# Turning the normalised rows of a one-core transformer kernel: scaled rows and transposes in place of a product with a diagonal

## What is computed

```python
def rms_norm(x, g, eps=NORM_EPS):
    xf = x.astype(F32)
    y = xf * lax.rsqrt(jnp.mean(xf * xf, axis=-1, keepdims=True) + eps)
    return (y * g.astype(F32)).astype(x.dtype)

for layer in range(DEPTH_2):
    h = swiglu_ffn(rms_norm(x, g[0]), ffn_w_gu[layer, 0], ffn_w_down[layer, 0])
    x = x + HALF_STEP * rms_norm(h, g[1])
    h = rms_norm(x, g[2])
    ...
    x = x + rms_norm(h, g[3])
    h = swiglu_ffn(rms_norm(x, g[4]), ffn_w_gu[layer, 1], ffn_w_down[layer, 1])
    x = x + HALF_STEP * rms_norm(h, g[5])
```

## Time and profile before

| | |
|---|---|
| median of 3 runs | 2836.6 us (2833.71 to 2836.64) |
| profiled execution, its own time | 2834.07 us |
| its span | 2832.3 us |
| mean granted TensorE clock | 0.981 |
| TensorE matmul busy | 2712.9 us, 96%, 19782 records |
| VectorE busy | 1760.8 us, 62% |
| ScalarE busy | 1419.7 us, 50% |
| GpSimd busy | 138.0 us, 5% |

### The profile page before, as it was taken

How to read it: one execution, slowest core, us unless ns; L and a number is a source line. 1 busy time by engine, 2 the same in 40 slices (tenths; PEclk the granted TensorE clock), 3 DMA queues, 4 the chain that set the end, 5 groups by cost and what they waited for, 6 DMA issues and landing times.

```text
span 2832.3 us, 47861 instructions
## 1 busy us (share of the span) xinstructions
PE 2712.9 (96%) x19782; PEld 2445.5 (86%) x19782; DVE 1760.8 (62%) x2118; ACT 1419.7 (50%) x1872; POOL 138.0 (5%) x206
## 2 busy tenths in 40 slices
PE   7899999899999999988998999999999999999999
PEld 7789999788888888878897888889988888888887
DVE  5555788665556665568655656566656566555655
ACT  5544577544545455456324445444345455455544
POOL 3000000000000000000301000000000000000000
PEclk9989999999999999999999999999999999999999
DMA  7165899555535545543203555555445545553553
GB/s 204 44 216 173 277 354 352 190 193 182 155 122 178 185 167 201 187 146 105 92 4 105 190 181 195 188 183 174 155 155 190 188 168 196 193 157 106 184 188 124
DMA packets 371293, 491.97 MB, mean 174 GB/s; under 512 B 12313, under 2 KB 331377, under 8 KB 371121
## 3 DMA queue, kind: packets, MB, share of 16 engines
q1 hardware_dynamic: 367968, 479.51, 50.5%
q0 software_dynamic: 2576, 7.97, 1.0%
q10 hardware_dynamic: 576, 1.98, 0.2%
HBM read 488.38 MB, written 1.05 MB: 173 GB/s over the span
## 4 chain that ended last, share of the span: by engine, by line
PE 88%; DVE 5%; ACT 4%; issue 1%; POOL 1%; DMA 0%; ACTq 0%; POOLq 0%; DVEq 0%
PE bank L351 21%; PE bank L350 11%; PE bank L330 9%; PE bank L331 9%; PE bank L332 9%; PE acc L330 7%; PE acc L332 7%; PE acc L331 7%; PE bank L2872 1%; ACT w_hi L295 1%; PE acc L604 1%; DVE X L509 1%; PE bank L2849 1%; DVE act_both L530 1%; PE bank L2860 1%
## 5 line engine op out<-in xcount | busy, mean ns | idle before, releaser
L300 DVE TENSOR_TENSOR w_lo<-raw,w_hi 128x2048 fp32r<-128x2048 f32 x360 | 824.1, 2292 | 509.7 <-ACT w_hi L295 509.2
L295 ACT ACTIVATE w_hi<-raw 128x2048 fp32r<-128x2048 f32 x360 | 688.2, 1912 | 268.6 <-PE acc L332 229.2
L351 PE MATMUL bank<-act_both,w_hi 128*128 128x512 f32 x2560 | 654.7, 392 | 0.0
L351 PEld LDWEIGHTS bank<-act_both,w_hi 128*128 128x128 f32 x2560 | 465.2, 189 | 82.8
L350 PEld LDWEIGHTS bank<-act_both,w_lo 128*128 128x128 f32 x2560 | 349.1, 190 | 25.0
L330 PE MATMUL acc<-w_hi,mix_hi 128*128 128x512 f32 x928 | 363.8, 392 | 4.4 <-ACT att_probs L1175 2.2
L332 PE MATMUL acc<-w_hi,mix_lo 128*128 128x512 f32 x928 | 362.0, 390 | 0.0
L331 PE MATMUL acc<-w_lo,mix_hi 128*128 128x512 f32 x928 | 361.7, 390 | 0.0
L350 PE MATMUL bank<-act_both,w_lo 128*128 128x256 f32 x2560 | 356.8, 282 | 0.0
L738 ACT ACTIVATE scratch<-bank 128x256 f32<-128x256 f32 x320 | 122.3, 385 | 429.1 <-PE bank L351 422.6
L330 PE MATMUL bank<-act_both,w_hi 128*128 128x256 f32 x1032 | 298.8, 290 | 22.1 <-DVEq L2290 8.0
(11 more groups left out here) (512 smaller groups left out, 3867.3 us busy)
## 6 DMA issues: line engine op xcount, KB each, us to landing
raw<-in_ffn_w_gu SPq DMA_DIRECT2D x176, 1024.0 KB, 5.0
raw<-in_ffn_w_down SPq DMA_DIRECT2D x88, 1024.0 KB, 4.8
raw<-in_ml_w_in SPq DMA_DIRECT2D x24, 1024.0 KB, 5.2
raw<-in_rt_w_in SPq DMA_DIRECT2D x24, 1024.0 KB, 5.1
raw<-in_w_up SPq DMA_DIRECT2D x20, 1024.0 KB, 6.8
raw<-in_w_gate SPq DMA_DIRECT2D x19, 1024.0 KB, 6.3
raw<-in_w_down SPq DMA_DIRECT2D x18, 1024.0 KB, 6.0
moe_raw<-in_w_down SPq DMA_DIRECT2D x14, 1024.0 KB, 6.0
```

Source lines behind the costliest of these rows:

```text
L295: act.activation(w_hi[0:rows, slot, 0:size], raw[0:rows, slot, 0:size], ACT.Copy).then_inc(hi_made, 1)
L300: dve.tensor_tensor(w_lo[0:rows, slot, 0:size], raw[0:rows, slot, 0:size], w_hi[0:rows, slot, 0:size].bitcast(F32), ALU.subtract).then_inc ...
L351: return pe.matmul(bank[b][:, :], w_hi[:, slot, w], act_both[:, k, :], start=k == 0, stop=k == KT - 1)
```

## The change

ScalarE no longer makes a diagonal. `spread(t)` multiplies the row half `X[:, t]` by `rstd`, in two instructions of 512 columns, into `scratch[:, t]`, each with its own count on the semaphore `rows_scaled`. TensorE turns `scratch` with the transpose form of the matmul against the identity, and waits before k = 0 for the first half and before k = 4 for the second.

```diff
--- before.py
+++ after.py
@@ -196,7 +196,6 @@
         scratch = sb("scratch", [P, TT, D])
         silu_out = sb("silu_out", [P, 2, 2 * T])
         gated = sb("gated", [P, 2, 2 * T])
-        diag = gated[:, 0, 0:TT * P].rearrange("p (t c) -> p t c", t=TT)
         work0 = top[0]
         assert work0 < nc.sbuf_usable_end
 
@@ -227,7 +226,7 @@
         x_quarter = sem("x_quarter")
         x_summed_act, x_summed_dve = sem("x_summed_act"), sem("x_summed_dve")
         x_rstd = sem("x_rstd")
-        diag_ready = sem("diag_ready")
+        rows_scaled = sem("rows_scaled")
         turned = sem("turned")
         norm_hi = sem("norm_hi")
         normed = sem("normed")
@@ -446,7 +445,10 @@
 
             def spread(t):
                 act.wait_ge(x_rstd, 2 * c.x_stats + t + 1)
-                act.activation(diag[:, t, :], ident, ACT.Copy, scale=rstd[:, 2 + t:3 + t]).then_inc(diag_ready, 1)
+                for half in range(2):
+                    cols = slice(half * 512, half * 512 + 512)
+                    act.activation(scratch[:, t, cols], X[:, t, cols], ACT.Copy,
+                                   scale=rstd[:, 2 + t:3 + t]).then_inc(rows_scaled, 1)
 
             def high(t):
                 for j in range(KT // 2):
@@ -592,8 +594,9 @@
             return b[:, k % 2 * P:k % 2 * P + P]
 
         def pe_turn(pe, c, t, low=True):
-            pe.wait_ge(diag_ready, 2 * c.norms + t + 1)
             for k in range(KT):
+                if k % 4 == 0:
+                    pe.wait_ge(rows_scaled, 4 * c.norms + 2 * t + k // 4 + 1)
                 if k in (4, 6):
                     if t == 0:
                         pe_result_free(pe, c.n + k // 2)
@@ -601,7 +604,7 @@
                         pe.wait_ge(normed, 8 * c.lows + k // 2 + 1)
                     else:
                         pe.wait_ge(norm_hi, 8 * c.norms + k // 2 + 1)
-                last = pe.matmul(turn_place(c, t, k), X[:, t, k * P:k * P + P], diag[:, t, :], start=True, stop=True)
+                last = pe.transpose(turn_place(c, t, k), scratch[:, t, k * P:k * P + P], ident)
                 if k % 2:
                     last.then_inc(turned, 1)
```

## The result

| | before | after |
|---|---|---|
| median, both measured together | 2836.61 us | 2848.04 us |
| runs | 6, 2833.71 to 2837.43 | 6, 2846.36 to 2850.92 |
| profiled execution: own time, span | 2834.07, 2832.3 us | 2847.52, 2845.7 us |
| mean granted TensorE clock | 0.981 | 0.975 |

The ratio is 1.0043, with a 95% interval of 1.0032 to 1.0054: **slower by 11.4 us**, where 2843 (+8.4 on the profiled execution, +6.4 on the median) was forecast. The value lies inside the range of 2834 to 2850. One run of experiment 4, of 3840 us at a mean granted clock of 0.65, was in a slow state of the chip and is left out of its ratio.

A forecast was written before the change was run, and what follows sets the result against it. TensorE was taken to hold 88% of the chain, with ScalarE late in the first turn; +1.5 us of work and +6.9 of clock, +8.4 on 2834.1, gave 2842.5, rounded up to 2843; range 2834 to 2850.

The forecast's parts named there:

- Each float32 transpose is one record: In TensorE's turns: a transpose is one record, a diagonal product two, so a turn shrinks from 1.8 to 0.9 us.
- +0.85 us of ScalarE before the last square, passed on in full, six times (+5.1): Six half-product crossings keeping the high clock: ScalarE's two multiplies delay the last square and everything behind it, +5.1 us.
- Nothing in the four at the lower clock (0): Four half-product crossings with a slow second turn: the turn ends last, at about the same time as before, 4 x 0.
- Recurrent mixer -0.3: Crossing into the recurrent mixer: +0.85 us from ScalarE, -1.1 from its slow second turn, together -0.3.
- Three crossings without a normed output, -1.1 each: After the final norm, first crossing and into the experts: half the records shorten a slow turn, -3.3 us in all.
- The clock, +6.9: five of the six crossings that keep it now fall: Fewer records and longer idling make five more half-product crossings fall to the lower clock, 1.37 us each, +6.9.
- The sum: Whole kernel: +1.5 us without the clock and +6.9 with it, +8.4 on the profiled 2834.1, rounded up to 2843.
- None falls: Rival: no further crossing falls to the lower clock, transposes weighing like products; 2835.6 us, chance 0.25.
- Every crossing falls: Rival: turns of transposes count for nothing, so every crossing falls, some twice; 2846.5 to 2850 us, chance 0.25.
- Faster: Rival: the second multiply does not hold up the last square, so TensorE's shorter turn decides; 2825.7 us, chance 0.06.
- Two records: Rival: transposes are two records each, like the products, so no gain at TensorE; 2843.8 us, chance 0.02.

The follow-up runs named there:

- experiment 4: Kernel before, with scaled rows and transposes only in the three crossings without a normed output, the diagonal in the other eleven: 2835.48 us, ratio 0.9997.
- Experiment 1: Kernel before, with one unread ScalarE multiply of 512 columns added behind each diagonal: 2840.53 us against 2836.56, ratio 1.0011.
- experiment 11: Kernel before, with 64 unread transposes of the identity in TensorE's idle time after the final norm: one run, 2839.61 us, no ratio.
- 12: Kernel before, with 32 unread float32 products (64 records) in TensorE's idle time after the final norm: one run, 2842.89 us, no ratio.
- experiment 5: Changed kernel, with unread identity products filling TensorE's waits, 5 behind the first turn and 9 before the second: 2843.78 us against 2837.34, ratio 1.0023.
- 10: Changed kernel, VectorE scaling the first turn's rows in normed crossings, plus 3 and 9 unread products in those crossings' gaps: 2833.43 us, ratio 0.9986.
- experiment 8: Changed kernel, but in crossings with a normed output VectorE instead of ScalarE multiplies the first turn's rows: 2840.78 us, ratio 1.0011.
- experiments 2 and 3: Changed kernel with 16 records per turn: transposes replaced by identity products (2850.98 us, ratio 1.0056), or each transpose issued twice (2850.40 us, 1.0049).
- experiment 9: Kernel before, transposes only in the three crossings without a normed output, 8 unread products before the second turn in normed crossings: 2831.89 us against 2836.70, ratio 0.9977.

## Why the prediction was right, and where it was not

*Each float32 transpose is one record.* Right: 112 + 112 for 28 turns.

*+0.85 us of ScalarE before the last square, passed on in full, six times (+5.1).* The lateness is right to 0.02, the passing on is not. ScalarE's pause before it read the turned rows was treated as nothing; it took up part, and 0.68 was left, 6 x 0.68 = +4.1. The prediction's own rows show this pause: ScalarE is free near 1051.67 and reads at 1051.93. Experiment 1 shows the same by another length: 0.55 later, 0.35 passed on.

*Nothing in the four at the lower clock (0).* Wrong. The crossings themselves did get shorter (10.44 for 10.6 to 11.1), since the turn no longer ends last; but the clock then falls behind them, on the products. In the first crossing that falls in both kernels, the distance from the last output product to the 89th product behind the second turn went from 22.64 to 23.14 us, +0.5; two others that fall in both give +0.8 and +0.4. The fourth fell before and holds in the change, and two that held before fall now. It is counted below as +0.5 four times.

*Recurrent mixer -0.3.* Measured +0.64: its second turn's gain did not show, its first turn's loss did.

*Three crossings without a normed output, -1.1 each.* -0.91, -1.22 and -1.49, the sum right to 0.3. Experiment 4 has -3.1 from the same three.

*The clock, +6.9: five of the six crossings that keep it now fall.* **This is the step that failed in its place, though hardly in its size.** One more fell, not five (+1.2). The clock cost 7.6 us by the medians (11.4 less 3.8), so the total is near the 6.9, but not by the mechanism given; as far as it fits, that is luck. Between the two profiled executions the price came mostly elsewhere, +9.3 us: in two mLSTM steps, in the router and around the RWKV crossing. The forecast did not look at the narrow products there, in which the clock of the kernel before fell too. How much of the 9.3 is the change's is open, since experiments 11 and 12 have the slow router and the slow mLSTM steps without the change. That work missing from TensorE in the crossings lowers the clock is shown by experiment 5 (filling the waits took about 8 us away and left the crossings of half products as long as they were) and by 10 against 8 (7.3 us). Why this moves a fall that comes later was not found.

*The sum.* On the profiled execution +8.4 was forecast and +13.4 came; on the medians it was +6.4 and +11.4. On the profiled executions the 5 us are: clock +3.6 (1.2 + 9.3 for 6.9), the four low crossings +2.0, the mixer +0.9, the six -1.0, the three -0.3, which is 5.2 by rounded pieces. With another profiled execution of before the pieces would be others.

*The rivals.* "None falls", 2835.6, is out. "Every crossing falls", which takes a turn of transposes for nothing, 2846.5 to 2850, has the measured 2848.0 in its interval, and reasons that the runs contradict: half of the crossings did not fall, and experiments 11 and 12 show transposes raising the clock. A total that fits is no proof of a mechanism. "Faster", 2825.7, needed a last quarter that comes 1.2 us after the factor; it came before. "Two records" is refuted by the count.

*Still open.* Where in the kernel the clock's 7.6 us are lost, and how much of them is the halved records and how much the longer pauses. On the second, experiments 2 and 3 put the halved records near 2 us by subtraction, which is no more than such a rest can tell. Which falls of the clock a given edit moves cannot be told ahead from these traces.

## What to carry to other kernels

Put work on an engine ahead of its critical instruction and you pay its length less the pause that the engine had behind it: here 0.87 us became 0.68, and 0.55 became 0.35, at each of ten crossings. So ask which engine has the pause; VectorE had one in the same place (experiment 8), and 7 us of the loss were gone. And where TensorE waits inside a busy stretch, try to fill the wait with products that nobody reads, only there and not longer than the wait: with that, and the transposes only where nothing is normed, 2836.7 became 2831.9 us, while with the same fill also at crossings without a pause there was no gain to be seen (2836.5). And before the clock's price is put down to a place, compare that place in several traces of kernels that do not differ there.

## What was not expected of the hardware

- TensorE's clock fell in stretches in which TensorE was never idle: 48 products of 8 columns, back to back, took 5.17 us in the trace of before and 7.54 in that of the change, with windows that are 5.00 of 5.00 us busy, and 7.61 in experiment 11, which has the program of before in that place.
- The same kernel before, on one chip, ran between 2833.5 and 2846.0 us (the 21 runs beside experiment 9). The longer ones go with a lower mean granted clock: 0.975 to 0.977 for the five runs above 2841, 0.980 and 0.981 for the six below 2836. With 11 runs of an experiment against 21 to 33 of before the interval still reached 0.1%, or 2.8 us, to each side, so an effect of 2 us was not to be seen.
- The clock also falls at another point of the crossing: before, it fell 7.8 to 8.4 us behind the last output product, in the turn; in the changed kernel 8.9 to 10.9 us behind it, in the turn or after it. The same crossing in different kernels, with the same work to within half a microsecond, falls in one and holds in the other.
